# A hybrid conformer and sparse-attention step: index queries, scores and gate products in one stage, and later stages that begin in parts

## The reference, cut to what matters

```python
h = rmsnorm(x, g) * (1 + scale) + shift
z = h @ w_in       # splits: a (2048), gc, q, k, v, ga, qi (512), ki (64), wi (8), gm (2048)
u = a[:, :1024] * sigmoid(a[:, 1024:])
s = einsum('bqhd,bsd->bqhs', qi, ki_all) * 64 ** -0.5         # 8 index heads of 64
score = einsum('bqhs,bqh->bqs', relu(s), wi)                  # chunk-causal
_, idx = top_k(score, 256)
p = softmax(q . k_all[idx] * 64 ** -0.5 + rel_bias)           # 16 heads, 4 key groups
o = (p @ v_all[idx]) * silu(ga)
c = swish(layernorm(causal_conv31(u))) * silu(gc)
m = sigmoid(gm[:, :1024]) * (c @ w_conv_out) + sigmoid(gm[:, 1024:]) * (o @ w_attn_out)
y = x + gate * rmsnorm(m @ w_out, g_post)
```

## Time and profile before

| | us |
|---|---|
| median of 3 runs | 4002.53 (3999.56 to 4005.60) |
| the profiled execution | 4000.31 |
| its span in the trace | 3998.6 |

### The profile page before, as it was taken

The page is one execution under the profiler, slowest core; times in us unless marked ns, Lnnn a source line. Parts: engine busy times, 40 slices in busy tenths (PEclk is TensorE's granted clock), DMA queues, the critical chain, the costliest instruction groups (busy, mean ns, idle before and its releaser), DMA issues. The chain is left out here.

```text
span 3998.6 us, 49726 instructions
## 1 busy us (share of the span) xinstructions
PE 3515.4 (88%) x18895; PEld 2935.9 (73%) x18895; DVE 2774.2 (69%) x4292; ACT 1334.7 (33%) x1532; POOL 1208.3 (30%) x1043
## 2 busy tenths in 40 slices
PE   5967778999999999999845889989989995999698
PEld 1967558999999999999723555555555564999687
DVE  1410899999996999999056777778777785454343
ACT  2210567667400000000153555545555552000011
POOL 1223323443443000000004453463463341454200
PEclk9988899999999999999976999999999997999899
DMA  7583203755556444444533211201201103565443
GB/s 267 161 281 99 48 14 116 211 164 188 181 181 232 173 143 171 165 155 149 209 118 84 64 28 31 64 23 34 67 23 34 32 27 126 171 223 167 159 120 119
DMA packets 381304, 502.12 MB, mean 126 GB/s; under 512 B 47304, under 2 KB 287064, under 8 KB 380507
## 3 DMA queue, kind: packets, MB, share of 16 engines
q1 hardware_dynamic: 253211, 212.58, 18.1%
q10 hardware_dynamic: 114672, 237.76, 17.9%
q0 software_dynamic: 13264, 49.85, 3.5%
HBM read 306.67 MB, written 199.73 MB: 127 GB/s over the span
## 5 line engine op out<-in xcount | busy, mean ns | idle before, releaser
L1046 PE MATMUL psum<-ha,gt 128*128 128x352 f32 x8064 | 1313.0, 324 | 27.9 <-POOL gt L602 17.0
L1046 PEld LDWEIGHTS psum<-ha,gt 128*128 128x128 f32 x8064 | 1309.8, 189 | 30.9 <-POOL gt L602 17.5
L1187 DVE SCALAR_TENSOR_TENSOR cv<-cv,vecs,cv 128x1056 f32<-128x1056 f32 (+1 forms) x480 | 598.9, 1325 | 0.0
L1915 DVE TENSOR_TENSOR at_plo<-at,at 128x1024 fp32r<-128x1024 f32 (+2 forms) x308 | 391.0, 1271 | 144.9 <-ACT at L1815 144.0
L1744 PE MATMUL psum<-at,at 128*128 128x512 f32 (+5 forms) x688 | 338.9, 498 | 154.1 <-DVE at L1845 51.3
L1814 ACT ACTIVATE at<-psum 128x1024 f32<-128x1024 f32 (+2 forms) x308 | 293.1, 952 | 533.8 <-PE psum L1702 533.8
L613 PE MATMUL psum<-br,br 128*128 128x352 f32 x2304 | 374.9, 324 | 42.1 <-DVE br L2029 41.1
L613 PEld LDWEIGHTS psum<-br,br 128*128 128x128 f32 x2304 | 374.3, 189 | 42.5 <-DVE br L2029 41.3
L842 DVE TENSOR_SCALAR_CACHE_REDUCE gt<-sc,gt 128x1792 bf16<-128x1792 f32 (+5 forms) x325 | 383.2, 1246 | 1.2
L1084 ACT ACTIVATE gt<-psum 128x1056 f32<-128x1056 f32 x80 | 84.0, 1049 | 654.0 <-PE psum L1046 638.6
L1744 PEld LDWEIGHTS psum<-at,at 128*128 128x128 f32 x688 | 138.1, 201 | 220.7 <-issue 57.9
(11 more groups left out here) (231 smaller groups left out, 4974.1 us busy)
## 6 DMA issues: line engine op xcount, KB each, us to landing
scratch_ws<-gt ACTq DMA_DIRECT2D x112, 512.0 KB, 6.1
gt<-scratch_ws ACTq DMA_DIRECT2D x112, 512.0 KB, 4.9
gt<-in_w_in_dram ACTq DMA_DIRECT2D x56, 512.0 KB, 5.3
scratch_gm<-gt ACTq DMA_DIRECT2D x32, 528.0 KB, 3.1
br<-scratch_gm ACTq DMA_DIRECT2D x32, 528.0 KB, 3.6
scratch_m<-br POOLq DMA_DIRECT2D x32, 528.0 KB, 4.4
at<-scratch_q SPq DMA_DIRECT2D x128, 128.0 KB, 2.8
su<-in_ada_w_dram SPq DMA_DIRECT2D x6, 2048.0 KB, 22.8
```

What stands on the lines that cost most here:

```text
L1046: ins = nc.tensor.matmul(psum[b][:, j, 0:W // 3], wt[b][:, c, :], a[:, c, j * (W // 3):(j + 1) * (W // 3)], start=(c == 0 and k == 0), sto ...
L1187: ins = nc.vector.scalar_tensor_tensor(to[:, 0:width], mine[:, k_:k_ + width], tap, to[:, 0:width], ALU.mult, ALU.add)
L1915: nc.vector.tensor_tensor(plo[j % 3][:, 0:len(mine), 0:n], prob[j % 3][:, 0:len(mine), 0:n], phi[j % 3][:, 0:len(mine), 0:n].bitcast(F32), ...
```

## The change

1. **Rows.** The hidden parts of the first 8 tiles, and 32 columns of the ninth, are written into the SBUF that the later stage reads (`kept`); they aren't stored to DRAM. The norm is done in place.
2. **One stage** for index queries, scores and gate. The query psum is evicted by ScalarE as high part and by VectorE as low part, both stored (`qih`, `qil`); nothing splits queries afterwards. They are loaded by units of 4 heads, in 4 DMAs of 128 KB. A dot is a piece of at most 1024 columns, 192 of them, in two halves of psum[0]. Six gate blocks (`FRONT`, three gm pairs, 48 chunks) go to psum[1] between dots, and ScalarE evicts them between relus. Each half then has the order gm (3 pairs), u, the rest of gm, gc, ga, q. Gated products stand at steps 48 + 17 j.
3. **Attention.** Half of group 0's keys (1600 columns) is loaded and split first; the first near rows precede `group_bias(0)`; the parts of a next group stand within `nears`, between head 1 and head 2.
4. **Branch.** The first run's activations come in 8 chunks on ScalarE's queue, with high parts by ScalarE, low parts by VectorE and a wait for each in the first product. The last run is unrolled, and w_out's load (8 DMAs of 512 KB) and split, the gains and output tile 0's parts are done beside it.
5. **Output.** It starts with product 0 at once.

The core of the diff:

```diff
         parts = mem.layout("rw", [([P, NT + 1, D], F32), ([P, KC, ROWW], F32R), ([P, KC, ROWW], F32R)]
-                           + [([P, D], F32)] * 2 + [([P, KC, P], F32)] * 2 + [([P, KC, P], F32R)] * 4
+                           + [([P, KC, P], F32)] * 2 + [([P, KC, P], F32R)] * 4
                            + [([P, ROWW], F32)] * 2 + [([P, 3, P], F32)] * 2)
-        xn, h, hhi, hlo, stage, kt = parts[3:5], parts[5:7], parts[7:9], parts[9:11], parts[11:13], parts[13:15]
+        h, stage, kt = parts[3:5], parts[9:11], parts[11:13]
+        half_acts = [([P, KC, W], F32R)] * 2
+        kept = mem.layout("ha", half_acts, at=mem.high(half_acts))
+        assert mem.high(half_acts) >= mem.base + sum((int(np.prod(part.shape[1:])) * 4 + 63) // 64 * 64 for part in parts)
+        KEEP = W // P
+
+        def parts_of(t):
+
+            if t < KEEP:
+                return [part[:, :, t * P:(t + 1) * P] for part in kept]
+            return [parts[5 + t % 2][:], parts[7 + t % 2][:]]
...
             def high(t):
                 act.wait_ge(s_h, t + 1)
-                if t >= 2:
+                if t == 0:
+                    act.wait_ge(mem.s_bias, 16)
+                    act.wait_ge(mem.s_cache, 48)
+                if t >= KEEP + 2:
                     act.wait_ge(s_mm, t - 1)
-                    act.wait_ge(s_hid[t % 2], 32 * (t // 2))
-                nc.scalar.copy(hhi[t % 2][:], h[t % 2][:]).then_inc(s_hi, 1)
+                    act.wait_ge(s_hid[t % 2], 32 * ((t - KEEP) // 2))
+                if t == KEEP + 2:
+                    act.wait_ge(s_tail, 32)
+                nc.scalar.copy(parts_of(t)[0], h[t % 2][:]).then_inc(s_hi, 1)
...
                 tok = slice(t * P, t * P + n)
+                if t < KEEP:
+                    return
+                hi, lo = parts_of(t)
                 sp.wait_ge(s_lo, t + 1)
-                sp.dma_start(scr["hhi"][:, :, tok], hhi[b][:, :, 0:n].bitcast(F32)).then_inc(s_hid[b], 16)
-                sp.dma_start(scr["hlo"][:, :, tok], hlo[b][:, :, 0:n].bitcast(F32)).then_inc(s_hid[b], 16)
+                sp.dma_start(scr["hhi"][:, :, tok], hi[:, :, 0:n].bitcast(F32)).then_inc(s_hid[b], 16)
+                sp.dma_start(scr["hlo"][:, :, tok], lo[:, :, 0:n].bitcast(F32)).then_inc(s_hid[b], 16)
+                if t == KEEP:
+                    for part, mine in zip(kept, (hi, lo)):
+                        sp.dma_start(part[:, :, KEEP * P:W].bitcast(F32), mine[:, :, 0:W - KEEP * P].bitcast(F32)).then_inc(s_tail, 16)
 
...
+        QI, FRONT = 8, 6
+        early = [("gm", i) for i in range(FRONT // 2)]
+        order = (early + [("u", i) for i in range(KC)] + [("gm", i) for i in range(FRONT // 2, KC)]
+                 + [(kind, i) for kind in ("gc", "ga", "q") for i in range(KC // 2)])
+        pairs = [(half, kind, i) for half in range(2) for kind, i in order]
...
+        def pieces_of(t):
+
+            width = keys_of(t)[1]
+            n = -(-width // 1024)
+            return [(k * (width // n), width // n) for k in range(n)]
...
+        sizes = [w_ for t, g in units for h in range(QB) for _, w_ in pieces_of(t)]
+        chunks_after, seen = [], 0
+        for w_ in sizes:
+            seen += w_
+            chunks_after.append(min(FRONT * KC, (seen * (FRONT * KC + 4)) // sum(sizes)))
...
+            def beside(j):
+
+                n, c = QI + j // KC, j % KC
+                if c == 0:
+                    pe.wait_ge(pr.s_split, n + 1)
+                    pe.wait_ge(pr.s_read, n)
+                ins = chunk(psum[1], n % 2, c, ahi, alo)
+                if c == KC - 1:
+                    ins.then_inc(pr.s_mm, 1)
+
+            pe.wait_ge(s_kis, 2)
+            pe.wait_ge(pr.s_read, QI - 1)
+            count = done = 0
+            for k, (t, g) in enumerate(units):
+                key0, width = keys_of(t)
+                pe.wait_ge(s_q[k % 2], 64 * (k // 2 + 1))
+                for h in range(QB):
+                    for o, w_ in pieces_of(t):
+                        if count >= 2:
+                            pe.wait_ge(s_relu, count - 1)
+                        for at, m in widths(0, w_):
+                            keys = ki[:, key0 + o + at:key0 + o + at + m]
+                            nc.tensor.matmul(dots[count % 2][:, at:at + m], qhi[k % 2][:, h, :], keys, start=True, stop=False)
+                            ins = nc.tensor.matmul(dots[count % 2][:, at:at + m], qlo[k % 2][:, h, :], keys, start=False, stop=True)
+                        ins.then_inc(s_dot, 1)
+                        while done < chunks_after[count]:
+                            beside(done)
+                            done += 1
+                        count += 1
...
+                for h in range(QB):
+                    for o, w_ in pieces_of(t):
+                        if count < 2:
+                            act.wait_ge(s_qst[count], 128)
+                        else:
+                            act.wait_ge(s_acc, count - 1)
+                        act.wait_ge(s_dot, count + 1)
+                        nc.scalar.activation(relu[count % 2][:, 0:w_], dots[count % 2][:, 0:w_], ACT.Relu).then_inc(s_relu, 1)
+                        if KC * (done + 1) <= chunks_after[count]:
+                            evict(done // 2, done % 2)
+                            load(QI + done + 3)
+                            keep(done + 1)
+                            done += 1
+                        count += 1
...
-            dve.wait_ge(pr.s_split, BLOCKS)
-            gated_at = {52 + 17 * j: half_pairs + j for j in range(KC)}
+            dve.wait_ge(pr.s_split, QI + BLOCKS)
+            first_u = half_pairs + FRONT // 2
+            gated_at = {48 + 17 * j: first_u + j for j in range(KC)}
```

```diff
-            def nears(u):
+            def nears(u, piece=None):
...
                 for h in range(GROUP):
+                    if h == 2 and piece:
+                        piece(u // NTL + 1)
                     e = GROUP * u + h
...
             queries(0)
+            nears(0)
             group_bias(0)
-            nears(0)
             group_values(0)
             parts_of_group = {8: group_values, 9: lambda g: group_keys(g, 0), 10: lambda g: group_keys(g, 1), 11: group_high, 12: group_bias}
             for u in range(len(units)):
                 if u:
                     queries(u)
-                    nears(u)
-                if u % NTL in parts_of_group and u // NTL + 1 < KV:
-                    parts_of_group[u % NTL](u // NTL + 1)
+                    nears(u, parts_of_group.get(u % NTL) if u // NTL + 1 < KV else None)
...
+            for c in range(KC):
+                act.dma_start(acts[0][1][:, c, :].bitcast(F32), scr["c"][c * P:(c + 1) * P, 0:W]).then_inc(s_first[c], 16)
+
+            def first_high(c):
+                act.wait_ge(s_first[c], 16)
+                nc.scalar.copy(acts[0][0][:, c, :], acts[0][1][:, c, :].bitcast(F32)).then_inc(s_fhi, 1)
...
+            def load_out():
+
+                act.wait_ge(pr.s_mm, KC * LAST)
+                for c in range(KC):
+                    act.dma_start(out_raw[:, c, :], w["w_out"][0, c * P:(c + 1) * P, :]).then_inc(s_wout, 16)
...
+                if r == 0 and not is_later(i):
+                    for c in range(KC):
+                        first_high(c)
+                if r == LAST:
+                    if i == 0:
+                        load_out()
+                    if i == 1:
+                        out_high(range(0, 4))
+                    if i == 2:
+                        out_high(range(4, KC))
+                        gain_part(0)
+                        gain_part(1)
+                    if i == 3:
+                        act.wait_ge(s_m, 32)
+                        nc.scalar.copy(mhi[:], mlo[:].bitcast(F32)).then_inc(s_mhi, 1)
+                        gain_part(2)
+                        gain_part(3)
+            sections.run_unrolling_last(act, step)
...
+            def spread(k):
+
+                if k >= 2:
+                    pe.wait_ge(s_gain, k - 1)
+                stream, first = k // 2, 4 * (k % 2)
+                for c in range(4):
+                    last = nc.tensor.matmul(gains[k][:, c * P:(c + 1) * P],
+                                            mem.gate_g[:, first + c, stream:stream + 1].to_broadcast([P, P]),
+                                            mem.ident[:], start=True, stop=True)
+                last.then_inc(s_bc, 1)
+
             def step(r, i, before):
-                if not is_later(i):
-                    pe.wait_ge(s_acts, 2 * KC * (r + 1))
+                if not is_later(i) and r:
+                    pe.wait_ge(s_acts, 2 * KC * r)
                 for b in range(2):
-                    pr.product(pe, b, before, *acts[r % 2])
-            sections.run(pe, step)
+                    first = r == 0 and b == 0 and not is_later(i)
+                    pr.product(pe, b, before, *acts[r % 2], ready=s_flo if first else None)
```

(17 more changed lines are left out.)

618 lines of the change are left out of this document (318 added, 300 removed).

## The result

The changed kernel takes **3886.83 us** (median of 4 runs, 3885.48 to 3890.22) against 4004.07 for the kernel before in the same comparison: a ratio of 0.9712, 95% interval 0.9696 to 0.9727. It is faster by 117 us where 175 were forecast, and it stands 7 us above the stated range (3780 to 3880). The profiled execution has a span of 3886.2 us, 112.4 less than before.

What follows compares the result with a forecast made beforehand. TensorE was taken as near its limit in the gate stage, with idle time at the stage seams. Terms −33 + 24 − 70 − 38 − 24 − 34 = −175 took 4000.31 to 3825, with 2.2 for the median 3828 us; range 3780 to 3880.

Steps and rivals of the forecast that it cites:

- the weights bind: −14: Start of merged stage: with the first half kept on chip, the weight split at 263.35 sets the first query product, −14 us.
- Scores: Scores stage: 248 us instead of 223.9, 24 longer, with TensorE and ScalarE both fitting beside VectorE.
- (a): Scores: seven POOL weight splits beside VectorE's scoring slow it by 2.4 us a pair, 17 us.
- (b): Scores: six evictions on ScalarE between relus, each with four DMAs to issue, 2.7 us each, 16 us.
- term (c): Scores: handing round of buffers between three engines, 6 us.
- Rival 1: Scores stretch to 290 us because evictions and chunks stand before relus and dots: +42, 3870 us; chance 12%.
- Gate stage: Gate stage: six of 112 blocks done earlier, −70 us; VectorE is late next, by some 15 us.
- The groups' term of 33: Attention: next group's parts between head 1 and head 2 win 33 of 55 us lost at group changes.
- The start's −5: Attention: first product earlier by 5 us, with half of group 0's keys loaded and split first.
- rival 2: Attention: group changes give nothing, as the wait moves to VectorE's near rows; +33, 3861 us; chance 13%.
- Rivals 3, 4 and 6: 3: uncertain costs hidden, 3789, 13%. 4: scores' dot, relu, scoring run serially, 4141, 2%. 6: an edit fails, 3862, 4%.
- Rival 5: Scores: a POOL weight split stops VectorE for its whole 4.2 us, seven times; +13, 3841 us; chance 8%.

## Why the prediction was right or wrong

**Queries and first score (−33, measured −26).** The step "the weights bind: −14" was right about the binder and wrong about its time: it kept 263.35 for the split, though 16 loads and the key split had been moved in front of it. I costed them at nothing with "96 us before their use, which hides them". The 96 was wrong, too: they are issued from 249.56 and first used at 322.42, 73 us. But the step fails for another reason: it asks only when their data is needed, not what they hold up. It cost 10 us against the forecast of the first product, and 15.7 against the run that issues them later. The wait of the second relu for the last store, 7.4 us, I had missed; but removing it gave back 2 at most.

**Scores (+24, measured +53).** This is the step that failed. It priced the six blocks by their evictions and splits (terms (a) and (b), 33 us) and gave their 48 chunks on TensorE nothing: "both fit beside VectorE, TensorE with 20% to spare". Measured, the blocks cost 69 us: the evictions with all that hangs on them some 26 by the starts of the relus, not far from the 33, and the chunks some 43 where the sum has 0. A chunk drained ScalarE and VectorE behind it, and cost 1.01 us of its 1.49 in the tile read above. The sentence on spare time compared sums of busy time, which says nothing about work that is handed round in pieces.

The base of the sum, 209 us, agrees with the 207.7 without blocks, but partly by luck. VectorE was busy for only 179.9 of these: its fixed part per operation, 0.31 us by two groups of seven, came to 0.16 where a tile has two pieces (three of 1024 take 3.68 us), and its waits took the rest, some 28 us, for which the sum had only the 6 of term (c). Inside the 33, term (a) is wrong in kind. In the change a weight split falls where VectorE has no relu: beside the six splits three of its operations are longer than others of their width, by 0.2 to 0.4 us each. What VectorE loses there is waits for relus, 4.25 us in the row at 468.10. Rival 1 had the mechanism at 290 us and 12%; the stage came to 276.5, two thirds of the way there.

**Gate stage (−70, measured −64).** Right step by step: VectorE is late next, 14 us behind TensorE; the last weight split no longer waits; the product of the eighth pair, not the search, sets the end. Missing was the wait of 11 us for u's stored columns. But I never set that gain against the blocks' own price in the scores; no line of the prediction says what the six are worth alone. Measured, they gain 50 over none and cost 69. By the prediction's own terms they should have cost 33 and paid 70.

**Attention (−38, measured −17).** The groups' term of 33 came to 25 by the run that undoes it, and to 30 against the profiles in which the third change was not slowed; in the change's own it gave only 2.6 (97.2 against 99.8). So the mechanism and nearly the size were right, and 6 us of this miss are the one execution. The start's −5 came to +2: I had read the early key split and not the line behind it, a clearing that the set-up count waits for. Taking it out of the count showed that the early product would not have helped either. Some 5 us of this miss have no cause that a run shows.

**Branch (−24) and tail (−34).** Right in mechanism and size: −22 with the gain products in it, and −33.

**Rivals and chances.** Rival 1 happened in weaker form (28 of its 42 us), together with misses in attention (21) and at the first product that no rival had; the groups' own part of them, 8 of 33, is a quarter of rival 2 at most. The range held each rival alone and not several misses of one sign; the sum stands 7 us outside it. Rivals 3, 4 and 6 did not happen. Rival 5's mechanism is seen at the stage's start: POOL's subtract of 2.34 us takes 5.40 beside VectorE's of 5.00, and ends 2.2 us after it, as if it had waited for its end; it takes 2.34 when that is moved away. This agrees with the Trainium skill ("SBUF — State Buffer", section "Who interferes with whom"). In the scores with fine pieces it is seen from the other side: at 455.93 an operation of 640 takes VectorE 2.45 us beside POOL's multiply of 455.81, and 0.88 at 463.90 without it. In the change it costs next to nothing there, for VectorE has no relu to work on when the splits run.

## What to carry to other kernels

When work of one engine is moved into the gaps of another's stage, its price isn't read off the engine's spare time. Where three engines hand work round through two buffers, a piece in between holds up the others, and a large piece more than the same work in small ones: six blocks cost 69 us in 48 pieces and 44 in 144, for the same instructions. Price the other engines' share too: the six evictions, stores, loads and keeps in front of relus were some 26 of the 69. And moved work pays only down to the next engine's chain: compute both ends, and then how many blocks, since in fine pieces the first four paid and the last two did not. A load that is needed late is not free when it is issued first; put it behind the ones that are waited for.

## What the runs showed that I had not expected

- The same POOL subtract took 2.34 us alone and 5.40 and 5.47 us beside a VectorE subtract of 64 × 3136.
- Leaving out products slowed others: without the chunks TensorE's granted clock in the scores fell from 0.94 to 0.84, and it was at 0.50 for the last 20 us. The total of such a run understates what was left out.
- Scoring operations got cheaper by being cut. In a tile with one piece of 1024 three take 4.06 us, in a tile with two such pieces 3.68. In the first each waits for the one before it on the same columns, in the second for the one before that (`s_acc`, count less the number of pieces). That this is the cause is not shown by a run of its own. The timeline of VectorE without early blocks, in the first kind of tile:

```profile
426.45 4.06 DVE L1195 SCALAR_TENSOR_TENSOR gt<-gt,wi,gt 128x1024 f32<-128x1024 f32 x3 [0.17 <-ACT gt L1144]
```

- Stages that no edit touched differ between executions: attention by 8 us (1213.3 to 1221.3), the scores by 10 (274.9 to 285.2). In the longest of these scores the granted clock was lowest, 0.90 against 0.93 to 0.95. A gain of a few microseconds in one such stage needs more than one profile.
